# The modulation products of a two-stream trunk layer: VectorE multiply-adds behind the lead-in, column groups of TensorE in it

## The chip, the cores and the metric

One core of a Trainium2 chip. The metric is the time of one execution on the device in microseconds; the time before is the median of three runs.

## The reference, cut to what matters

One layer (D = 2048) runs over 128 context tokens and 256 sample tokens, T = 384 in all. Each stream has its own conditioning vector; both go through the same w_mod (2048 x 12288). The result is six rows of 2048 per stream: shift and scale for two norms, and two residual gates.

```python
m = silu(cvec) @ w_mod + b_mod                        # cvec: c_ctx for the context, c for the sample
hn = rmsnorm(x, g[0]) * (1.0 + mod[:, 1]) + mod[:, 0]
z = hn @ w_in                                         # 2048 x 5120
# x_lru, y_gate, b_g, c_g, v: convolution, gates, two scans, gated short convolution
x = x + mod[:, 2] * (concat(lru_out, sc_out) @ w_out) # 2048 x 2048
hn = rmsnorm(x, g[1]) * (1.0 + mod[:, 4]) + mod[:, 3]
f = (silu(hn @ w_gate) * (hn @ w_up)) @ w_down        # D_FF = 5632
x = x + mod[:, 5] * f
```

The outputs are both streams after a final rmsnorm and the last scan states of the context.

## The kernel before

**Products.** Activations lie transposed (features on partitions, 384 tokens in the free dimension). Every weight matrix is cut into blocks of 1024 elements a partition. A block arrives as fp32 in a `raw` slot; ScalarE rounds it to fp32r in `w_hi` (`round_blocks`, L427); VectorE subtracts, which gives the rest `w_lo` (`subtract_blocks`, L707); TensorE adds three products hi x hi, hi x lo, lo x hi (`product`, L1132 to L1134). A block of a large matrix is 24 matmuls of 384 columns (`gemm_block`). `w_hi` and `w_lo` have four slots, so block b can be rounded once TensorE is done with block b - 4. `raw` has four slots of 1 MB, two blocks each.

**Modulation.** w_mod is cut into 24 steps of 512 columns, each four quarters of 512 rows (1 MB). The two conditioning vectors are split into high and low parts, four stationary columns `cond_w`. A step is eight blocks; a block (`mod_block`, L1149) is four matmuls of 512 columns, so 32 a step, summed in rows 0 to 3 of `MOD_BANK`. VectorE copies the four rows to `mod_row` (`copy_row`, L713), TensorE turns them onto partitions and adds high and low with the matrix `select` (`turn_row`, L1166: four matmuls), and VectorE adds the bias into `modT` (`add_bias`, L719).

**Stages.** The lead-in holds product steps 0 to 7 (`mod_step`), which the first norm needs in full. In steps 1 to 4 x is transposed, the position embedding added (L821), and squares summed over features by matmuls against ones (L1221). Behind the root and its reciprocal (L734), POOL multiplies the eight pairs of tiles of x by it (L406). Then come 16 combined steps, GM 0 to 15 here (`gm_step`): ten over w_in (phases x, c, v, b, y, two steps each), four over w_out, one of w_gate and one of w_up. Each holds eight blocks of the large matrix, interleaved one to one with the eight blocks of one product step. In the w_in steps VectorE and ScalarE also do the convolutions (L849 to L858), gates and scans of one head a step (`powers`, `scans`); in the w_out steps the residual additions (L962) and sums of squares (L971). Steps 0 and 14 begin with a norm (`norm_tiles`, L762). Behind them the feed-forward runs in chunks without products.

**Order.** Every engine's order is written out by hand in one list per engine, with waits on counting semaphores: `lo_ready` (blocks subtracted), `block_done` (blocks used by TensorE), `landed` (per raw slot), `row_ready`, `row_turned`, `mod_ready`. SP issues all weight loads in order (L314). In a combined step even raw slots hold quarters of the large matrix and odd ones quarters of w_mod, and every load waits for `lo_ready`. In VectorE's list the row copy and the bias of step m stand in step m + 1.

Of the kernel before, what the change touches and what calls it, by code (L numbers as in the profile page):

```python
# [23 lines left out]
ALU = mybir.AluOpType  # L24
# [4 lines left out]
P = 128  # L29
# [34 lines left out]
def build(nc, x_prompt, x_sample, state_rglru, c, c_ctx, w_mod, b_mod, norm_g, w_in, lru_conv_w, lru_conv_b,  # L64
# [46 lines left out]
    N_IN = MOD_FIRST * 8  # L111
    N_OUT = N_IN + IN_STEPS * 16
    N_G0 = N_OUT + OUT_STEPS * 16
    N_U0 = N_G0 + 16
    N_G1 = N_U0 + 16
# [8 lines left out]
    with ExitStack() as ctx:  # L124
# [19 lines left out]
        mod_row = sb("mod_row", [4, BANK])  # L144
# [4 lines left out]
        cond_w = sb("cond_w", [P, KT, 4], F32R)  # L149
# [6 lines left out]
        state_rows = sb("state_rows", [2 * HEADS, P])  # L156
        select = sb("select", [4, 2])
# [54 lines left out]
        block_done = sem("block_done")  # L212
        zeroed = sem("zeroed")
# [5 lines left out]
        cond_hi_ready = sem("cond_hi_ready")  # L219
# [55 lines left out]
        def raw_of(kind, block):  # L275

            if kind == "GM":
                quad, at = divmod(block, 4)
                half, second = at % 2, at // 2
                wide = half == 1  # L280
            else:
                quad, at = divmod(block, 4)
                half, second = divmod(at, 2)
                wide = kind != "G"
            slot = 2 * (quad % 2) + half
            if not wide:
                return slot, raw[slot][:].rearrange("p (k n) -> p k n", n=256)[:, 4 * second:4 * second + 4, :]
            view = raw[slot][:].rearrange("p (k n) -> p k n", n=512)
            if kind == "D":
                return slot, view[:, :, 256 * second:256 * second + 256]  # L290
            return slot, view[:, 2 * second:2 * second + 2, :]

        def split_view(tile, kind, block):
            n = 512 if kind == "M" or (kind == "GM" and block % 2) else 256
            return tile[slot_of(block)][:].rearrange("p (k n) -> p k n", n=n)

        def landed_by(n, block):

            return (n - block) * 2 + 16 * (block // 8) + 16
# [5 lines left out]
        def _(sp):  # L305
            def quad(n, quad_at, halves, apart=False):


                first = 2 * (quad_at % 2)
                for half, source in enumerate(halves):  # L310
                    if not isinstance(n, int) or n >= 8:
                        sp.wait_ge(lo_ready, n - 6 + 2 * half if apart else n - 4)
                    width = source.shape[2]
                    sp.dma_start(raw[first + half][:].rearrange("p (k n) -> p k n", n=width), source)\  # L314
                        .then_inc(landed[first + half], 16)
# [5 lines left out]
            def mod_half(at, quarter):  # L321
                return w_mod_v[:, 4 * quarter:4 * quarter + 4, bass.ds(at, 512)]
# [5 lines left out]
            def gm_step(n, view, col, m, k_order=(0, 1)):  # L328
                at = held(m * 512)
                for q in range(4):  # L330
                    quad(n + 4 * q, q, [g_half(view, col, q, k_order), mod_half(at, q)])

            def g_step(n, view, col, apart=True):
                col = held(col)
                for q in range(2):
                    quad(n + 4 * q, q, [g_half(view, col, 2 * q), g_half(view, col, 2 * q + 1)], apart=apart)

            def d_step(n, chunk):
                first_k = held(chunk * CHUNK)
                for q in range(2):  # L340
                    quad(n + 4 * q, q, [w_down_v[:, bass.ds(first_k, CHUNK), 1024 * q + 512 * h:1024 * q + 512 * h + 512]
                                        for h in range(2)], apart=True)

            def m_step(n, m):
                at = held(m * 512)
                for q in range(2):
                    quad(n + 4 * q, q, [mod_half(at, 2 * q), mod_half(at, 2 * q + 1)], apart=True)

            m_step(0, 0)
# [3 lines left out]
            with sp.Fori(1, MOD_FIRST) as i:  # L353
                m_step(i * 8, i)
            for phase, (_, col) in enumerate(PHASES):
                with sp.Fori(0, 2) as i:
                    gm_step(i * 16 + N_IN + 32 * phase, w_in_v, i * 512 + col, i + (MOD_FIRST + 2 * phase))
            with sp.Fori(1, OUT_STEPS + 1) as i:
                gm_step(i * 16 + (N_OUT - 16), w_out_v, i * 512 - 512, i + (MOD_FIRST + IN_STEPS - 1), k_order=(1, 0))
            gm_step(N_G0, w_gate_v, 0, MOD_STEPS - 2)  # L360
            gm_step(N_U0, w_up_v, 0, MOD_STEPS - 1)
            g_step(N_G1, w_gate_v, 512, apart=False)
# [20 lines left out]
            sp.dma_start(new_state[0, 0].rearrange("a (h e) -> (a h) e", e=P), state_rows[:]).then_inc(stored, 16)  # L383
# [4 lines left out]
        def _(pool):  # L388
            for g, group in enumerate(groups[1:], 1):
# [6 lines left out]
            pool.dma_start(select[:], tables[0:4, POS + P:POS + P + 2]).then_inc(tables_landed, 16)  # L396
# [23 lines left out]
        def _(act):  # L420
            def round_blocks(kind, n, blocks):
                for b in blocks:
                    slot, source = raw_of(kind, b)
                    act.wait_ge(landed[slot], landed_by(n + b, b))
                    if not isinstance(n, int) or n + b >= SLOTS:
                        act.wait_ge(block_done, n + b - (SLOTS - 1))
                    act.activation(split_view(w_hi, kind, b), source, ACT.Copy).then_inc(hi_ready, 1)  # L427
# [27 lines left out]
            act.wait_ge(silu_ready, 1)  # L455
# [921 lines left out]
```

## Time and profile before

| | |
|---|---|
| median of three runs | 1910.89 us (1910.23 to 1910.91) |
| profiled execution, span of its core from first to last instruction | 1910.3 us |
| TensorE, VectorE, ScalarE, POOL busy | 1840.8, 1041.2, 794.7, 40.1 us |
| mean granted TensorE clock | 0.982 of full |
| DMA | 307.34 MB, mean 161 GB/s |
| lead-in | 0 to 131.9 us |
| combined steps GM 0 to 15 | 131.9 to 856.1 us |
| feed-forward and end | 856.1 to 1910.3 us |

The profiled execution's own time is given by its span; no separate time of it is listed beside the three runs. Step boundaries are read from the timeline: a step starts where VectorE's first subtraction of it has ended and TensorE takes up its first block. PE is TensorE's matmuls, PEld its weight loads; a matmul's duration overlaps the next one's, so starts are compared where a rate is meant. An fp32 matmul leaves two records, an fp32r matmul one.

### The profile page before, as it was taken

The page shows a single profiled execution, that of the slowest core. Times are in us where ns is not written, and L with a number is a line of the kernel's source. Part 1 is how long each engine was busy: PE and PEld are TensorE (multiplying, and loading weights), DVE is VectorE, ACT ScalarE, POOL GpSimd, SP SyncE. Part 2 cuts the span into 40 slices and gives each one's busy share as a digit, 9 for nine tenths or more (in the row PEclk, how much of TensorE's full clock was granted, in tenths as well). Part 3 has the DMA queues.
Part 4 walks back from the last instruction along what each step waited for, and adds up shares of the span by engine and source line. Part 5 has one row for each costly group of instructions (what it writes and reads, how often), then busy time and mean ns, then how long its engine had stood idle before and what let it go on. Part 6 is the DMA issues. An engine that isn't in the chain of part 4 may idle for free.

```text
span 1910.3 us, 25615 instructions
## 1 busy us (share of the span) xinstructions
PE 1840.8 (96%) x10189; PEld 1692.1 (89%) x10189; DVE 1041.2 (55%) x1380; ACT 794.7 (42%) x870; POOL 40.1 (2%) x43
## 2 busy tenths in 40 slices
PE   5979999999999998899999999999999999999997
PEld 2438888888888887789999999999999999999997
DVE  6887655775557556753434353535353534444445
ACT  5755455555676444642222222222222222222225
POOL 1040000000000000000000000000000000000000
PEclk9969999999999999999999999999999999999998
DMA  9956566556655565464333333433343334333321
GB/s 356 320 197 213 184 203 204 181 184 194 205 186 176 182 214 176 160 214 133 126 118 131 132 124 117 132 132 122 120 132 132 118 124 132 132 116 126 132 89 67
DMA packets 226464, 307.34 MB, mean 161 GB/s; under 512 B 5229, under 2 KB 152993, under 8 KB 226033
## 3 DMA queue, kind: packets, MB, share of 16 engines
q1 hardware_dynamic: 225008, 304.11, 46.8%
q0 software_dynamic: 1200, 2.52, 0.8%
q8 instruction: 29, 0.48, 0.1%
q14 instruction: 19, 0.15, 0.0%
q10 hardware_dynamic: 208, 0.08, 0.0%
HBM read 303.54 MB, written 3.15 MB: 161 GB/s over the span
## 4 chain that ended last, share of the span: by engine, by line
PE 89%; DVE 7%; ACT 2%; issue 1%; DMA 0%; ACTq 0%; DVEq 0%
PE psum L1132 26%; PE psum L1134 26%; PE psum L1133 26%; PE psum L1155 4%; PE psum L1156 4%; DVE w_lo L707 3%; PE psum L1166 1%; PE psum L1252 1%; ACT w_hi L427 1%; PE psum L1221 1%; DMA ident<-in_tables 0%; DVE act_lo L762 0%; DVE mod_row L713 0%; DVE scratch L747 0%; DVE scratch L918 0%
## 5 line engine op out<-in xcount | busy, mean ns | idle before, releaser
L707 DVE TENSOR_TENSOR w_lo<-raw,w_hi 128x1024 fp32r<-128x1024 f32 x568 | 695.7, 1243 | 820.7 <-ACT w_hi L427 819.8
L427 ACT ACTIVATE w_hi<-raw 128x1024 fp32r<-128x1024 f32 x568 | 587.5, 1056 | 1001.6 <-PE psum L1134 946.5
L1132 PE MATMUL psum<-act_hi,w_hi 128*128 128x384 f32 x2304 | 779.2, 338 | 20.2 <-DVE act_lo L762 15.2
L1134 PE MATMUL psum<-act_hi,w_lo 128*128 128x384 f32 x2304 | 773.6, 336 | 0.0
L1133 PE MATMUL psum<-act_lo,w_hi 128*128 128x384 f32 x2304 | 772.5, 335 | 0.0
L1132 PEld LDWEIGHTS psum<-act_hi,w_hi 128*128 128x128 f32 x2304 | 434.4, 189 | 42.7 <-issue 17.1
L1133 PEld LDWEIGHTS psum<-act_lo,w_hi 128*128 128x128 f32 x2304 | 434.5, 189 | 6.2
L1134 PEld LDWEIGHTS psum<-act_hi,w_lo 128*128 128x128 f32 x2304 | 434.0, 188 | 0.0
L1132 PE MATMUL psum<-h_hi,w_hi 128*128 128x384 f32 x704 | 235.7, 335 | 0.9 <-DVE h_lo L1025 0.9
L1134 PE MATMUL psum<-h_hi,w_lo 128*128 128x384 f32 x704 | 235.2, 334 | 0.0
L1133 PE MATMUL psum<-h_lo,w_hi 128*128 128x384 f32 x704 | 235.2, 334 | 0.0
L1155 PE MATMUL psum<-w_hi,cond_w 128*4 128x512 f32 x384 | 159.7, 416 | 24.4 <-DVE mod_row L713 17.0
L1156 PE MATMUL psum<-w_lo,cond_w 128*4 128x512 f32 x384 | 158.0, 411 | 0.0
L1132 PEld LDWEIGHTS psum<-h_hi,w_hi 128*128 128x128 f32 x704 | 132.1, 188 | 1.2 <-DVE h_lo L1025 1.2
L1133 PEld LDWEIGHTS psum<-h_lo,w_hi 128*128 128x128 f32 x704 | 132.2, 188 | 0.0
L1134 PEld LDWEIGHTS psum<-h_hi,w_lo 128*128 128x128 f32 x704 | 132.1, 188 | 0.0
L1034 DVE SCALAR_TENSOR_TENSOR xT<-psum,modT,xT 128x128 f32<-128x128 f32 x352 | 122.1, 409 | 7.0 <-PE psum L1134 6.9
L1155 PEld LDWEIGHTS psum<-w_hi,cond_w 128*4 128x4 f32 x384 | 33.2, 86 | 74.6 <-DVE w_lo L707 20.2
L1156 PEld LDWEIGHTS psum<-w_lo,cond_w 128*4 128x4 f32 x384 | 33.6, 87 | 47.5 <-issue 7.9
L613 ACT ACTIVATE h_hi<-stage 128x768 fp32r<-128x768 f32 x22 | 18.6, 846 | 48.1 <-DVE stage L1020 48.1
L1166 PEld LDWEIGHTS psum<-select,mod_row 4*128 4x128 f32 x192 | 23.9, 192 | 10.4 <-issue 8.7
L1166 PE MATMUL psum<-select,mod_row 4*128 4x2 f32 x192 | 25.9, 253 | 2.0 <-DVE mod_row L713 1.1
(129 smaller groups left out, 578.3 us busy)
## 6 DMA issues: line engine op xcount, KB each, us to landing
raw<-in_w_mod SPq DMA_DIRECT2D x96, 1024.0 KB, 7.3
raw<-in_w_gate SPq DMA_DIRECT2D x44, 1024.0 KB, 5.1
raw<-in_w_up SPq DMA_DIRECT2D x44, 1024.0 KB, 5.1
raw<-in_w_down SPq DMA_DIRECT2D x44, 1024.0 KB, 5.0
raw<-in_w_in SPq DMA_DIRECT2D x40, 1024.0 KB, 5.2
raw<-in_w_out SPq DMA_DIRECT2D x16, 1024.0 KB, 5.3
stage<-in_x_sample SPq DMA_DIRECT2D x2, 1024.0 KB, 15.9
y_sample<-stage SPq DMA_DIRECT2D x4, 512.0 KB, 4.7
```

What stands on the lines that cost most here:

```text
L427: act.activation(split_view(w_hi, kind, b), source, ACT.Copy).then_inc(hi_ready, 1)
L613: act.activation(h_hi[:, 2 * pair:2 * pair + 2, :], silu_g[:, 2 * pair:2 * pair + 2, :], ACT.Copy)\
L707: dve.tensor_tensor(split_view(w_lo, kind, b), source, split_view(w_hi, kind, b).bitcast(F32), ALU.subtract).then_inc(lo_ready, 1)
L1034: last = dve.scalar_tensor_tensor(xT[:, k, start:end], psum[:, down_banks[j] + a, start:end], modT[:, 5 * KT + k, seg:seg + 1], xT[:, k, s ...
L1132: pe.matmul(psum[:, bank, 0:T], hi, x_hi, start=first, stop=False)
L1133: pe.matmul(psum[:, bank, 0:T], hi, x_lo, start=False, stop=False)
L1134: return pe.matmul(psum[:, bank, 0:T], lo, x_hi, start=False, stop=last)
L1155: pe.matmul(psum[0:4, MOD_BANK, :], cond_w[:, k, :], hi[:, kk, :], start=k == 0, stop=False)
L1156: out = pe.matmul(psum[0:4, MOD_BANK, :], cond_w[:, k, :], lo[:, kk, :], start=False, stop=k == KT - 1)
L1166: out = pe.matmul(psum[:, SMALL_BANK, 2 * a:2 * a + 2], mod_row[:, a * P:(a + 1) * P], select[:], start=True, stop=True)
L1221: out = pe.matmul(psum[:, SUM_BANK, 0:T], ones[:], x_squares[:, a, :], start=four == 1 and a == 0, stop=four == 4 and a == 3)
L1252: out = pe.matmul(psum[:, bank, 0:T], gate_w[:, which, :], mix[:, bass.ds(head, 1), :].rearrange("p a t -> p (a t)"), start=True, stop=True)
```

## The change

- In the lead-in a product quarter is no longer rounded and split. TensorE reads the fp32 quarter from its raw slot with the unsplit fp32 `cond_w`, padded to 32 columns of which two are not zero. Its four 128-row pieces go to the four 32-column groups of the array and to four groups of 32 partitions of `MOD_BANK`: four fp32 matmuls of 512 columns a quarter, 16 a step. `copy_row` copies 128 partitions; `select` adds the groups.
- In the combined steps VectorE makes the products: `mod_quarter` multiplies and adds 4 x 2 times 512 elements a quarter into `mod_sum` (128 partitions, two streams), each waiting for the product before the last one. `turn_sum` sums over partitions with eight fp32 matmuls of one column against `ones`.
- A new semaphore `mod_used` counts used quarters. SP waits for it before it loads the next quarter into the slot.
- A combined step has 8 instead of 16 blocks to round and subtract, so the block counts and the places in all lists change. A memset of `cond_w` stands first in POOL's list.
- `state_rows` lies in `gate_w`, `mod_row` in `mod_sum`.

```diff
+            def load(slot, source):
+
+                width = source.shape[2]
+                sp.dma_start(raw[slot][:].rearrange("p (k n) -> p k n", n=width), source).then_inc(landed[slot], 16)
...
+                for q in range(4):
+                    slot = 2 * (q % 2)
+                    if first and q < 2:
+                        sp.wait_ge(mod_used, m * 4 - 4 + slot + 1)
+                    else:
+                        sp.wait_ge(lo_ready, n + (2 * q - 2))
+                    load(slot, g_half(view, col, q, k_order))
+                    if first and q < 2:
+                        sp.wait_ge(mod_used, m * 4 - 4 + slot + 2)
+                    else:
+                        sp.wait_ge(mod_used, m * 4 + (q - 1))
+                    load(slot + 1, mod_quarter(at, q))
...
+            def m_step(m):
                 at = held(m * 512)
+                for q in range(4):
+                    if not isinstance(m, int) or m:
+                        sp.wait_ge(mod_used, m * 4 + (q - 3))
+                    load(q, mod_quarter(at, q))
...
+            pool.memset(cond_w[:], 0.0).then_inc(cond_zeroed, 1)
...
+            def mod_quarter(m, q):
+
+                slot = 2 * (q % 2) + 1
+                dve.wait_ge(landed[slot], m * 32 + 16 * (q // 2 + 1 - MOD_FIRST))
+                rows = raw[slot][:].rearrange("p (k n) -> p k n", n=512)
+                if q:
+                    dve.wait_ge(mod_used, m * 4 + q)
+                for kk in range(4):
+                    k = 4 * q + kk
+                    for which in range(2):
+                        total, weight = mod_sum[:, which, :], cond[:, which, k:k + 1]
+                        if kk:
+                            dve.wait_ge(own.sem, own.value - 1)
+                        if k == 0:
+                            last = dve.tensor_scalar(total, rows[:, kk, :], weight, None, ALU.mult)
+                        else:
+                            last = dve.scalar_tensor_tensor(total, rows[:, kk, :], weight, total, ALU.mult, ALU.add)
+                        if kk < 3 or which == 0:
+                            own.add(last)
+                last.then_inc(mod_used, 1)
...
-                    subtract_blocks("GM", n, range(0, 2))
+                    subtract_blocks("GM", n, range(0, 1))
                     if head >= 1:
                         scans(head - 1)
...
+                    subtract_blocks("GM", n, range(1, 2))
+                    drain_pair(before, 2 * ((step - 1) % 2) + 1, 2, n)
+                    subtract_blocks("GM", n, range(2, 4))
+                    add_bias(m - 1)
+                mod_quarter(m, 0)
+                subtract_blocks("GM", n, range(4, 5))
+                mod_quarter(m, 1)
+                drain_pair(phase, 2 * turn, 0, n + 4)
+                subtract_blocks("GM", n, range(5, 7))
+                mod_quarter(m, 2)
                 if head >= 0:
                     powers(head)
-                subtract_blocks("GM", n, range(15, 16))
+                subtract_blocks("GM", n, range(7, 8))
+                mod_quarter(m, 3)
...
-            def mod_block(n, kind, b, k0):
...
+            def mod_quarter(q, slot, landing):
+
+                pe.wait_ge(landed[slot], landing)
+                rows = raw[slot][:].rearrange("p (k n) -> p k n", n=512)
+                for j in range(4):
+                    out = pe.matmul(psum[32 * j:32 * j + 32, MOD_BANK, :], cond_w[:, 4 * q + j, :], rows[:, j, :],
+                                    start=q == 0, stop=q == 3, tile_position=(0, 32 * j))
+                out.then_inc(mod_used, 1)
...
+            def turn_sum(m):
+
+                pe.wait_ge(mod_used, m * 4 + 4)
+                for a in range(4):
+                    for which in range(2):
+                        out = pe.matmul(psum[:, SMALL_BANK, 2 * a + which:2 * a + which + 1],
+                                        mod_sum[:, which, a * P:(a + 1) * P], ones[:, 0:1], start=True, stop=True)
+                out.then_inc(row_turned, 1)
```

The w_out, w_gate and w_up steps have the same pattern of quarters and blocks; step 0 and step 14 have their first quarter behind the norm tiles.

## Rows read from the trace of the kernel before

**Rows 1.** The page: busiest engine, and the chain that ended last.

```profile
PE 1840.8 (96%) x10189; PEld 1692.1 (89%) x10189; DVE 1041.2 (55%) x1380; ACT 794.7 (42%) x870; POOL 40.1 (2%) x43
...
PE 89%; DVE 7%; ACT 2%; issue 1%; DMA 0%; ACTq 0%; DVEq 0%
```

**Rows 2.** Windows of the lead-in: window, length, busy us per engine (x instructions), clock, DMA.

```profile
0.00:29.90 29.90, 10.14 (x36) 3.52 (x36) 14.46 (x33) 14.60 (x18) 6.66 (x18) 0.95 0.97 360
22.00:30.00 8.00, 0.79 (x5) 0.42 (x3) 4.84 (x23) 5.04 (x7) 0.00 (x0) 0.82 1.03 382
29.90:82.80 52.90, 49.50 (x232) 23.87 (x232) 45.30 (x57) 38.92 (x40) 0.75 (x1) 0.96 0.93 326
82.80:95.80 13.00, 11.38 (x48) 4.96 (x48) 11.27 (x10) 10.08 (x11) 0.00 (x0) 1.00 0.96 339
95.80:117.00 21.20, 14.57 (x36) 4.16 (x36) 21.01 (x9) 7.50 (x8) 21.16 (x9) 0.57 0.53 177
117.00:131.90 14.90, 13.14 (x45) 4.34 (x44) 11.16 (x12) 7.34 (x7) 1.46 (x2) 0.69 0.72 245
```

**Rows 3.** Windows behind it, columns as before: GM steps 0, 1, 2-3, 4-6, 7-8, 9-10, 11-13, 14, 15.

```profile
131.90:183.50 51.60, 46.53 (x245) 41.91 (x246) 40.40 (x58) 35.23 (x51) 0.00 (x0) 0.93 0.59 201
183.50:227.10 43.60, 43.60 (x240) 38.30 (x239) 30.62 (x41) 18.03 (x25) 0.00 (x0) 1.00 0.56 193
227.10:316.10 89.00, 89.00 (x482) 77.34 (x481) 55.37 (x68) 51.93 (x60) 2.88 (x4) 1.00 0.58 191
316.10:451.70 135.60, 133.99 (x722) 115.81 (x721) 96.39 (x138) 77.72 (x90) 4.31 (x6) 1.00 0.58 192
451.70:542.00 90.30, 90.11 (x486) 77.86 (x485) 54.28 (x63) 57.41 (x65) 2.88 (x4) 1.00 0.58 191
542.00:630.00 88.00, 84.17 (x450) 72.84 (x449) 57.04 (x65) 52.74 (x59) 0.00 (x0) 0.98 0.55 190
630.00:756.00 126.00, 126.00 (x698) 111.55 (x696) 73.76 (x92) 53.18 (x55) 0.00 (x0) 1.00 0.60 201
756.00:814.30 58.30, 45.69 (x237) 39.20 (x236) 43.43 (x58) 36.23 (x46) 0.00 (x0) 0.91 0.44 151
814.30:856.10 41.80, 41.80 (x233) 37.04 (x233) 21.46 (x20) 17.48 (x19) 0.00 (x0) 1.00 0.61 202
```

**Rows 4.** Timeline of TensorE, step 3: start us, length us; product matmuls.

```profile
273.26 0.40 PE L1155 MATMUL psum<-w_hi,cond_w 128*4 128x512 f32 x1
273.49 0.40 PE L1156 MATMUL psum<-w_lo,cond_w 128*4 128x512 f32 x1
```

**Rows 5.** Chain in order of time: row turning, and four fp32 matmuls (two records each).

```profile
46.48 2.58 PE psum L1221 x8
...
239.16 0.98 PE psum L1166 x8
```

**Rows 6.** Timeline near the end: three fp32 matmuls of one column.

```profile
1897.54 1.33 PE L1334 MATMUL psum<-ones,sumsq 128*128 128x1 f32 x6 [1.31 <-DVE sumsq L1105]
```

**Rows 7.** Groups by shape, VectorE: busy us, mean ns, idle before.

```profile
L707 DVE TENSOR_TENSOR w_lo<-raw,w_hi 128x1024 fp32r<-128x1024 f32 x568 | 695.7, 1243 | 820.7 <-ACT w_hi L427 819.8 <-DVE rstd L734 0.2
...
L713 DVE COPY mod_row<-psum 4x512 f32<-4x512 f32 x24 | 16.2, 674 | 3.1 <-PE psum L1156 3.0
...
L854 DVE SCALAR_TENSOR_TENSOR scratch<-scratch,prm 128x386 f32<-128x386 f32 x24 | 14.9, 621 | 0.8
...
L858 DVE SCALAR_TENSOR_TENSOR stage<-scratch,prm 128x256 f32<-128x256 f32 x16 | 7.7, 480 | 0.0
```

**Rows 8.** Timeline of VectorE, step 11: four multiply-adds of 128, 256, 128, 256 elements.

```profile
654.49 1.38 DVE L962 SCALAR_TENSOR_TENSOR xT<-psum,modT,xT 128x128 f32 x4
```

**Rows 9.** Timelines of POOL and of VectorE, end of the lead-in.

```profile
95.84 21.15 POOL L406 TENSOR_TENSOR stage<-xT,rstd 128x768 f32<-128x768 f32 x8 [18.14 <-DVE rstd L734]
...
99.25 18.82 DVE L707 TENSOR_TENSOR w_lo<-raw,w_hi 128x1024 fp32r<-128x1024 f32 x7
```

**Rows 10.** Timeline of VectorE, step 14: last norm tiles.

```profile
787.42 1.82 DVE L762 TENSOR_TENSOR act_lo<-scratch,act_hi 128x768 fp32r<-128x768 f32 x2
```

More of the change, by code:

```diff
@@ L305, in _, with mod_quarter @@
         def _(sp):
[L306 to L315, printed above, removed]
+            def load(slot, source):
+                width = source.shape[2]
+                sp.dma_start(raw[slot][:].rearrange("p (k n) -> p k n", n=width), source).then_inc(landed[slot], 16)
             def held(value):
                 return value if isinstance(value, int) else sp.snap(value)
-            def mod_half(at, quarter):
+            def mod_quarter(at, quarter):
                 return w_mod_v[:, 4 * quarter:4 * quarter + 4, bass.ds(at, 512)]
@@ L338, in d_step, with g_step @@
+            def g_step(n, view, col, first=False):
+                col = held(col)
+                for slot in range(SLOTS):
+                    if first and slot % 2:
+                        sp.wait_ge(mod_used, MOD_STEPS * 4 - 2 + slot // 2 + 1)
+                    elif first:
+                        sp.wait_ge(lo_ready, n - 2 + slot)
+                    else:
+                        sp.wait_ge(lo_ready, n + (2 * slot - 6))
+                    load(slot, g_half(view, col, slot))
             def d_step(n, chunk):
@@ L339, in d_step @@
                 first_k = held(chunk * CHUNK)
[L340 to L344, printed above, removed]
+                for slot in range(SLOTS):
+                    sp.wait_ge(lo_ready, n + (2 * slot - 6))
+                    load(slot, w_down_v[:, bass.ds(first_k, CHUNK), 512 * slot:512 * slot + 512])
@@ L504, in gelu @@
                     act.activation(gelu_y, banks(bank), ACT.Gelu_apprx_tanh).then_inc(gelu_ready, 1)
-                round_blocks("GM", n, range(0, 4 if step else 2))
+                round_blocks("GM", n, range(0, 2 if step else 1))
                 if step == 0:
@@ L975, in out_step @@
             def out_step(n, i, first):
-                subtract_blocks("GM", n, range(0, 3))
-                copy_row(None, n)
-                if not first:
-                    subtract_blocks("GM", n, range(3, 4))
+                subtract_blocks("GM", n, range(0, 2))
+                m = i + (MOD_FIRST + IN_STEPS)
                 if first:
@@ L1195, in turn_params, with mod_step @@
                                  ident[0:rows, 0:rows]).then_inc(turned, 1)
-            def mod_step(m, blocks=range(8)):
-                if blocks[0] == 0 and (not isinstance(m, int) or m):
+            def mod_step(m, quarters=range(4)):
+                if quarters[0] == 0 and (not isinstance(m, int) or m):
                     pe.wait_ge(row_ready, m)
-                for b in blocks:
-                    mod_block(m * 8 + b, "M", b, 2 * b)
-                    if b == 4 and (not isinstance(m, int) or m):
+                for q in quarters:
+                    mod_quarter(q, q, m * 16 + 16)
+                    if q == 2 and (not isinstance(m, int) or m):
                         turn_row(m - 1)
```

322 lines of the change are left out of this document (144 added, 178 removed).

## The prediction

> **What bounds the kernel now.** I read the page first, then the chain of waits, then windows cut at the steps, then shapes and single timelines. On the page TensorE is busy 96% of the span and the chain that ended last lies on it for 89% [rows 1]. That average hides two regimes, and the windows separate them. In the lead-in (0 to 131.9 us, product steps 0 to 7) DMA is busy over 90% until 95.8, so the loads almost set the pace; then comes a stretch at 53% with a granted clock of 0.57 [rows 2]. There POOL's eight multiplications take 21.15 us and VectorE needs 18.82 us for seven subtractions, 2.7 us each instead of 1.24: the two slow each other, TensorE waits, and DMA waits with it [rows 7, 9]. Behind the lead-in the 16 combined steps (GM 0 to 15) run from 131.9 to 856.1 with TensorE busy nearly throughout, VectorE between 51% and 78% [rows 3]. From 856.1 to the end nothing changes except one row turning.
>
> The sum is made against the profiled execution, span 1910.3 us; the median of the three runs is 1910.89, 0.6 above, which I add at the end.
>
> **TensorE behind the lead-in.** A step loses 32 product matmuls. They start 0.23 us apart [rows 4], so 7.4 us. Its row turning (four matmuls, 0.98 us [rows 5], 0.245 each) becomes eight one-column matmuls against ones. No row shows eight in a stream. Below, the price of the four turning matmuls gives 8 x 0.245 = 1.96; above, three such matmuls took 1.33 us [rows 6], so 3.5. The turning is nearest in being pipelined, so 1.96. TensorE needs 6.4 us less a step.
>
> **VectorE behind the lead-in.** A step loses eight subtractions and one row copy and gains 32 products of 128x512, 30 of them multiply-adds. No row has that width. Multiply-adds of 386 and 256 elements last 0.621 and 0.480 us [rows 7], 1.085 ns an element, so 512 elements last 0.758. What counts in a queue is start to start. Four multiply-adds took 1.38 us, the last a 256-element one of 0.48: three starts in 0.90 for 512 elements, or 0.556 for elements and 0.115 fixed for each [rows 8, 7]. So 0.556 + 0.115 = 0.67 us a product. Each waits only for the product before the last (two accumulators alternate), which ended before it could start. Bounds: 0.60 (nearly no fixed part) and 0.79 (0.758 and a semaphore's turn). 32 x 0.67 = 21.4 us; off go 8 x 1.15 (1.243 less the same overlap of 0.09) and 0.6 for the copy: VectorE needs 11.6 us more a step. The two products of a step that are plain multiplications may save 0.5; I leave that for lost handovers.
>
> The Trainium skill's page "VectorE: DVE Perf Modes", section "The DRAIN you can't avoid", says that the next operation does not start until the pipe is empty. Here the four in rows 8 are shorter together than their durations, so the trace speaks against a full drain; by the rule a product costs 0.758, and that is the second rival below.
>
> **Step by step**, the larger of VectorE (busy + 11.6 a step) and TensorE (busy - 6.4 a step) [rows 3]:
> - step 1: 30.6 + 11.6 = 42.2, before 43.6;
> - steps 2-3: 55.4 + 23.2 = 78.6 (TensorE 76.2), before 89.0;
> - steps 4-6: 96.4 + 34.8 = 131.2, before 135.6. Two convolution drains a step make VectorE the bound; TensorE idles in lumps of some 6 us;
> - steps 7-8: 77.5 (TensorE 77.3), before 90.3;
> - steps 9-10: 80.2, before 88.0;
> - steps 11-13: 108.6 (TensorE 106.8), before 126.0.
>
> That is 518.3 against 572.5: 54 us off. Half of what TensorE gets back is lost again, because VectorE arrives at the same moment.
>
> Step 0 gets longer. VectorE's 40.4 + 11.6 = 52.0, and about 3.5 at its start when it waits for the row to be turned and for ScalarE's first scaled tile: 55.5 against 51.6, +4. There the products queue behind the norm tiles and ahead of blocks 4, 5 and 7 of the weights.
>
> Step 14 has a serial head (sum of squares, root, norm tiles) that stays. Its last norm tile ends at 789.2 [rows 10]; three subtractions and the row copy fewer ahead of it make that 785.2. Then 21.4 of products, four subtractions (4.6) and step 15's first (1.15) give 812.4 against 814.3: 2 off. Step 15 has VectorE 33.1, TensorE 35.4 against 41.8: 6 off. The next turning costs 1 more.
>
> **Queues.** SP's loads of product quarters now wait for VectorE's products and stand in front of weight loads. Walked through: blocks 6 and 7 of a step are issued once its first quarter is used, some 8 us before their rounding; 1.05 MB takes 2.7 us at full rate [rows 2], two of them 5.5. It fits, with 1 to 2 us to spare. ScalarE loses eight roundings a step and was no bound (35.2 of 51.6 at most [rows 3]); it hides at nothing behind TensorE. POOL gets a memset ahead of its parameter loads; I take up to 1 us at the first row, covered by the loads under way.
>
> **The lead-in.** It must load eight product steps and x: 8 x 4.19 + 3.15 = 36.7 MB. By 29.9 us 10.8 MB are in [rows 2]. The full rate is 382 GB/s (window 22 to 30, share 1.03). The other 25.9 MB take 67.8 us: 97.7. A quarter frees its slot as soon as TensorE has used it, no rounding or subtraction between, so I let the rate hold, with 1.5 for a gap where step 1 starts, 0.9 for the last quarter and 2 for stretches at the lower clock: the last row is complete at 102 instead of 131.9, 30 off. A quarter is four fp32 matmuls of 512 columns; four of 384 take 2.58 us in all [rows 5], 0.645 each, so 0.86. If the four column groups run together a quarter takes 0.86, otherwise 3.44. The loads bring a quarter each 2.7. No row shows column groups. The same skill's page "TensorE: Matmul & The Clock Gate", Part 3, gives a measured 2.38x for three column tiles; by that a quarter would take about 1.5, an estimate, and the sum stays. POOL is ready: step 5 starts near 66 instead of 82.8, POOL began 13.0 behind that start [rows 2, 9], and its 21.15 (less, uncontended) end by 100.
>
> **Sum:** 30 - 4 + 54 + 2 + 6 - 1 = 87 off 1910.3 is 1823.3; with 0.6, 1824.
>
> **Rivals.**
> 1. The column groups do not run together: the change doesn't do what it says there. A quarter is 3.44, a step 13.8. Steps 1 to 4 add the x work, (49.5 - 4 x 7.4) / 4 = 5.0 each [rows 2], 18.8; steps 5 to 7 add 1 of turning and once 2.6 of squares, 47.0. From 29.6 the row is complete at 151.8, 50 later than forecast: 1874. For it: no fp32 matmul in column groups in the trace. 14%.
> 2. A product costs its full 0.758: 0.088 x 32 = 2.8 us a step; in step 15 TensorE hides it, so 15 x 2.8 = 42 more, 1866; at 0.79 it would be 58, 1882. Against: rows 8. 16%.
> 3. Slower than before. In the lead-in the groups run one after the other and the clock stays at its lower level, as it fell to 0.57 and 0.69 where TensorE waited on others [rows 2]. A quarter is then T = 6.9, and the other work of rival 1 doubles: the row is complete at 29.6 + 28 T + 40 + 11 = 274, 172 later than forecast, and the kernel takes 1996. All that is won elsewhere is 57, so this decides from a last row at 189, T = 3.9 us, on. Against it: an engine that computes all the time had a clock of 1.00 [rows 3]. 4%.
> 4. Better: a product at 0.60 takes 2.2 off each step that VectorE bounds and leaves TensorE the bound in steps 2, 3, 7, 8 and 11 to 13 (22 in all), and the lead-in runs without its 3.5 of allowance: 1798.
>
> **Numbers.** Forecast (1798 to 1850, the products between 0.60 and 0.72, rival 4 at its end) 64%, rival 1 14%, rival 2 16%, rival 3 4%, anything else that leaves no gain 2%. The range 1800 to 1878 takes in the forecast and rivals 1 and 2 in most of their width. The measurement tells about 0.2% (4 us) from no change. Faster 0.95, same 0.01, slower 0.04.
>
> **What would show it.** Lead-in windows at 370 GB/s or more and first norm near 102; fp32 product matmuls of a quarter starting together and ending within 0.9 us (else rival 1); products 0.67 apart, 32 a step, VectorE over 90% in steps 1 to 13; steps of about 39 in 2, 3, 7, 8, of 46 to 47 in step 5; TensorE idle before blocks 5 and 7 in steps 4 to 6, released by subtractions; the part behind 856.1 unchanged in length. Wrong would be: TensorE's clock low for long after those idle lumps, or SP's loads late so that ScalarE's rounding waits on DMA.

## The result and the profile after

The changed kernel takes 1934.8 us (median of four runs, 1933.7 to 1935.7) against 1910.6 for the one before in the same runs: a ratio of 1.0124, interval 1.011 to 1.0138. It is slower by 24 us where 87 less was forecast. The two profiled executions, spans 1934.0 and 1910.3, are compared below.

The page of the changed kernel: busy time and chain, to be read beside [rows 1].

```profile
PE 1750.1 (90%) x9805; PEld 1676.3 (87%) x9805; DVE 1125.9 (58%) x1683; ACT 602.9 (31%) x678; POOL 33.7 (2%) x44
...
PE 68%; DVE 17%; DMA 7%; issue 5%; ACT 3%; SPq 0%; DVEq 0%; ACTq 0%
```

TensorE has 91 us less to do, VectorE 85 us more, and neither is full: the chain goes back and forth between them. The windows say where (columns as in [rows 2, 3]): two of the lead-in, then GM steps 0, 1, 2-3, 4-6, 7-8, 9-10, 11-13, 14, 15. Here each is cut where TensorE starts a step's first block; step 13 so includes the head of the second norm.

```profile
22.00:95.00 73.00, 57.11 (x328) 24.50 (x328) 15.07 (x38) 10.18 (x10) 14.86 (x9) 0.80 1.04 382
95.00:111.40 16.40, 7.94 (x45) 3.43 (x41) 4.64 (x12) 4.14 (x7) 1.52 (x3) 0.60 1.07 366
111.40:159.10 47.70, 40.13 (x192) 39.49 (x193) 45.38 (x70) 21.55 (x32) 0.00 (x0) 0.82 0.49 159
159.10:207.20 48.10, 40.80 (x213) 39.81 (x212) 40.10 (x63) 10.89 (x20) 0.00 (x0) 0.89 0.56 184
207.20:301.10 93.90, 81.71 (x435) 77.55 (x433) 75.15 (x109) 37.05 (x46) 2.88 (x4) 0.95 0.54 180
301.10:449.70 148.60, 122.17 (x651) 113.80 (x649) 128.08 (x207) 53.61 (x66) 4.31 (x6) 0.94 0.53 174
449.70:544.00 94.30, 81.96 (x433) 77.15 (x433) 75.66 (x109) 41.23 (x49) 2.88 (x4) 0.95 0.56 184
544.00:638.40 94.40, 78.23 (x420) 75.16 (x420) 82.13 (x120) 37.20 (x43) 0.00 (x0) 0.95 0.55 178
638.40:787.50 149.10, 116.79 (x643) 112.07 (x643) 115.43 (x178) 34.63 (x39) 0.00 (x0) 0.93 0.56 183
787.50:834.70 47.20, 37.97 (x193) 35.82 (x193) 44.15 (x65) 22.92 (x30) 0.00 (x0) 0.93 0.41 133
834.70:879.10 44.40, 37.65 (x209) 36.49 (x209) 31.81 (x44) 9.94 (x10) 0.00 (x0) 0.96 0.58 191
```

Cut in the same way, the kernel before begins step 0 at 138.0 and leaves step 15 at 856.1; the changed one does so at 111.4 and 879.1. So the lead-in gave 26.6 us, the sixteen steps took 49.6 more (767.7 instead of 718.1), and the rest is as long as it was (1054.9 and 1054.2). All of the loss lies in the combined steps, where 58 less was forecast. In steps 1 to 13 and 15 neither TensorE (78 to 87% busy) nor VectorE (72 to 87%) has a busy time near the window's length: that points to a handover, not a volume. Steps 0 and 14 are different: there VectorE is busy 45.4 of 47.7 and 44.2 of 47.2 us.

The waits of the changed kernel in the combined steps 1 to 13, 159 to 780 us (who waited for whom: us in total, times, longest):

```profile
PE psum L1160 <- DVE w_lo L718: 91.3, 47, 7.0
DVE modT L751 <- PE psum L1201: 83.1, 13, 8.4
```

VectorE waits once a step at the bias (L751) for the row to be turned (L1201), 6.4 us each time in the mean, and TensorE then waits for subtractions. One round of it, from step 3 of the changed kernel: the timeline of VectorE, that of SP, and of TensorE the first large matmul of the next step (timeline) and the next turning (chain in order of time):

```profile
268.85 0.17 DVE L751 TENSOR_TENSOR modT<-psum,prm 128x8 f32<-128x8 f32 x1 [6.88 <-PE psum L1201]
268.93 0.87 DVE L740 TENSOR_SCALAR mod_sum<-raw,cond 128x512 f32<-128x512 f32 x2
269.72 4.06 DVE L742 SCALAR_TENSOR_TENSOR mod_sum<-raw,cond,mod_sum 128x512 f32<-128x512 f32 x6
273.70 1.22 DVE L718 TENSOR_TENSOR w_lo<-raw,w_hi 128x1024 fp32r<-128x1024 f32 x1
...
284.07 1.22 DVE L718 TENSOR_TENSOR w_lo<-raw,w_hi 128x1024 fp32r<-128x1024 f32 x1 [1.85 <-ACT w_hi L443]
...
294.10 5.39 DVE L742 SCALAR_TENSOR_TENSOR mod_sum<-raw,cond,mod_sum 128x512 f32<-128x512 f32 x8
299.40 1.22 DVE L718 TENSOR_TENSOR w_lo<-raw,w_hi 128x1024 fp32r<-128x1024 f32 x1
...
307.67 1.23 DVE L718 TENSOR_TENSOR w_lo<-raw,w_hi 128x1024 fp32r<-128x1024 f32 x1 [0.27 <-ACT w_hi L443]
315.77 0.17 DVE L751 TENSOR_TENSOR modT<-psum,prm 128x8 f32<-128x8 f32 x1 [6.87 <-PE psum L1201]
```

```profile
273.94 0.37 SPq L306 DMA_DIRECT2D raw<-in_w_mod  x1
274.56 0.37 SPq L306 DMA_DIRECT2D raw<-in_w_in  x1
```

```profile
301.10 0.63 PE L1160 MATMUL psum<-act_hi,w_hi 128*128 128x384 f32 x1
...
314.05 1.69 PE psum L1201 x16
```

Read it as a loop. `mod_quarter(m, 0)` overwrites `mod_sum`, which `turn_sum(m - 1)` reads; so the bias and the first product stand behind the turning. From the bias at 268.85 VectorE works through four quarters of products and four subtractions to the next step's first subtraction, done at 300.6: 31.8 us. TensorE is through with the old step and with the gate matmuls at about the same time, starts block 0 at 301.1, is done with blocks 0, 1 and 2 at 314.05 (13.4 us after VectorE's subtraction) and turns the row until 315.74, 1.7 us. Only then does VectorE go on: 31.8 + 13.4 + 1.7 = 46.9, the length of the step (from bias to bias, 268.85 to 315.77). VectorE's subtractions and scans beside TensorE's three blocks fill only part of the 13.4, and TensorE's blocks 3 to 7 are fed one by one behind products. Both engines are on the path, one after the other.

### The profile page after: what moved, and what is told of

The parts are those of the page before. It is cut to its first block, busy times and chain, and to the rows that moved or that the text cites. A ratio compares the mean times of both kernels' runs of the same rounds, so it can differ in the third digit from the quotient of the medians.

```text
span 1934.0 us, 24719 instructions
## 1 busy us (share of the span) xinstructions
PE 1750.1 (90%) x9805; PEld 1676.3 (87%) x9805; DVE 1125.9 (58%) x1683; ACT 602.9 (31%) x678; POOL 33.7 (2%) x44
## 4 chain that ended last, share of the span: by engine, by line
PE 68%; DVE 17%; DMA 7%; issue 5%; ACT 3%; SPq 0%; DVEq 0%; ACTq 0%
PE psum L1160 22%; PE psum L1161 21%; PE psum L1162 21%; DVE mod_sum L742 9%; DMA raw<-in_w_in 3%; DMA raw<-in_w_mod 3%; DVE w_lo L718 2%; PE psum L1201 1%; PE psum L1182 1%; ACT w_hi L443 1%; DVE mod_sum L740 1%; ACT scratch L457 1%; DVE scratch L872 1%; DMA raw<-in_w_gate 0%; ACT act_hi L461 0%
## 5 line engine op out<-in xcount | busy, mean ns | idle before, releaser
L1160 PE MATMUL psum<-act_hi,w_hi 128*128 128x384 f32 x2304 | 797.8, 346 | 132.0 <-DVE w_lo L718 112.3
L718 DVE TENSOR_TENSOR w_lo<-raw,w_hi 128x1024 fp32r<-128x1024 f32 x376 | 458.3, 1224 | 596.1 <-ACT w_hi L443 595.4
L1161 PE MATMUL psum<-act_lo,w_hi 128*128 128x384 f32 x2304 | 787.0, 342 | 0.0
L1162 PE MATMUL psum<-act_hi,w_lo 128*128 128x384 f32 x2304 | 786.4, 341 | 0.0
L443 ACT ACTIVATE w_hi<-raw 128x1024 fp32r<-128x1024 f32 x376 | 394.6, 1058 | 998.8 <-PE psum L1162 687.1
L1160 PEld LDWEIGHTS psum<-act_hi,w_hi 128*128 128x128 f32 x2304 | 445.5, 193 | 156.9 <-DVE w_lo L718 126.0
L1161 PEld LDWEIGHTS psum<-act_lo,w_hi 128*128 128x128 f32 x2304 | 446.0, 194 | 0.5
L742 DVE SCALAR_TENSOR_TENSOR mod_sum<-raw,cond,mod_sum 128x512 f32<-128x512 f32 x480 | 323.3, 745 | 0.0
L751 DVE TENSOR_TENSOR modT<-psum,prm 128x8 f32<-128x8 f32 (+1 forms) x24 | 4.0, 166 | 128.2 <-PE psum L1201 94.2
L1182 PE MATMUL psum<-raw,cond_w 128*32 128x512 f32 x256 | 43.5, 783 | 23.8 <-DMA raw<-in_w_mod 19.0
L1182 PEld LDWEIGHTS psum<-raw,cond_w 128*32 128x32 f32 x256 | 6.5, 124 | 47.4 <-DMA raw<-in_w_mod 19.7
L624 ACT ACTIVATE h_hi<-stage 128x768 fp32r<-128x768 f32 x22 | 18.6, 846 | 48.1 <-DVE stage L1041 48.1
L1201 PEld LDWEIGHTS psum<-ones,mod_sum 128*128 128x128 f32 x256 | 30.8, 192 | 1.2 <-DVE mod_sum L742 1.2
```

Of the source, the lines that this page charges most:

```text
L443: act.activation(split_view(w_hi, b), source, ACT.Copy).then_inc(hi_ready, 1)
L718: dve.tensor_tensor(split_view(w_lo, b), source, split_view(w_hi, b).bitcast(F32), ALU.subtract).then_inc(lo_ready, 1)
L742: last = dve.scalar_tensor_tensor(total, rows[:, kk, :], weight, total, ALU.mult, ALU.add)
L1160: pe.matmul(psum[:, bank, 0:T], hi, x_hi, start=first, stop=False)
L1161: pe.matmul(psum[:, bank, 0:T], hi, x_lo, start=False, stop=False)
L1162: return pe.matmul(psum[:, bank, 0:T], lo, x_hi, start=False, stop=last)
```

## The experiments

Each is one edit of the changed kernel unless it says otherwise; before was measured beside each at 1910.7 to 1911.6.

**1. Where the row is turned.** The turning moves from ahead of the 4th block to ahead of the 1st, 2nd or 3rd.

```diff
-            def gm_step(n, m, bank_free, acts=None, k_order=(0, 1), turn_at=3, gates=None, pair_banks=(0, 2)):
+            def gm_step(n, m, bank_free, acts=None, k_order=(0, 1), turn_at=0, gates=None, pair_banks=(0, 2)):
```

> The changed kernel with one edit: TensorE turns the previous step's row ahead of a combined step's first block instead of ahead of its fourth. Theory A (VectorE's bias waits for that turning, 6.9 us in each step, and the first product quarter and all behind it are late by as much): steps 2 and 3 fall from 46.9 to about 40, the wait before the bias (94 us in all) falls below 20, and the kernel takes about 1855 (1840 to 1875). Theory B (loads of blocks 6 and 7 stand in SP's queue behind the wait for the first product quarter): the stall moves to the rounding, gain under 20, above 1915. Theory C (VectorE has more work in a step than TensorE, throughput): the wait before the bias was slack that VectorE would need anyway, gain under 20.

> The changed kernel with the turning ahead of a step's third block instead of its fourth: half of the dose of the run that turns first. Theory A (each block ahead of the turning is 4.2 us that VectorE waits in each of 13 steps): 13 x 4.2 = 54 less than the changed kernel, about 1880 (1870 to 1890), between it and the 1840 of turning first. Theory B (loads) or a threshold in the queue: no change by itself, or all of the gain at once.

> One edit against the changed kernel: the row of the step before is turned ahead of the 2nd block (the change has it ahead of the 4th; the 3rd gave 1876.6 us, the 1st 1840.5). Theory (VectorE stands still at the bias until the row is turned, and TensorE's block is 4.2 us, so each block the turning moves forward takes 4.2 us off a wait of 6.9 us): 2.7 us of wait were left ahead of the 3rd block and none is left ahead of the 2nd; and ahead of the 1st block TensorE waits for VectorE's last product (7.7 us in 159 to 780), which the block now ahead of the turning covers. So 1835 us (1828 to 1842). Rival (what counts is that the row is handed over as early as can be, since VectorE needs all the lead that it can get): between the two neighbours, about 1856 (1848 to 1866).

| turned ahead of block | median us | ratio, interval | bias waits | TensorE waits for w_lo |
|---|---|---|---|---|
| 4th (the change) | 1934.8 | 1.0124, 1.011 to 1.0138 | 83.1 | 91.3 |
| 3rd | 1876.6 | 0.9816, 0.980 to 0.9833 | 29.7 | 55.7 |
| 2nd | 1840.6 | 0.9636, 0.962 to 0.9653 | 1.6 | 36.3 |
| 1st | 1840.5 | 0.9627, 0.9611 to 0.9643 | none | 23.7 |

The waits are those of 159 to 780 us, row for row. For the 3rd and the 2nd block:

```profile
PE psum L1160 <- DVE w_lo L718: 55.7, 30, 5.0
DVE modT L751 <- PE psum L1201: 29.7, 10, 4.2
```

```profile
PE psum L1160 <- DVE w_lo L718: 36.3, 28, 4.5
DVE modT L751 <- PE psum L1201: 1.6, 1, 1.6
```

Each block of some 4.2 us that the turning moves forward comes off the bias's wait until that is gone, and the kernel gets 58, 36 and 0 us faster. A handover moved by one argument is worth 94 us. The 1st place came out 15 us better than the theory's 1855, at the edge of its range; the 3rd fell near its 1880. The 2nd place fell where the theory put it (1828 to 1842), not at the rival's 1856.

**2. The load order.** SP issues the last weight load of a step (blocks 6, 7) ahead of the load of the third product quarter, which waits for VectorE to use the first one.

```diff
+                weights(2)
+                weights(3)
+                products(2)
+                products(3)
```

(in place of weights and products in turn; the first two pairs stay as they are)

> The changed kernel with one edit: SP issues the load of blocks 6 and 7 ahead of the load of the third product quarter, so it no longer waits until VectorE has used the first quarter. Theory A: only the 1.9 us that the subtraction of block 6 waited go away, 1915 to 1930. Theory B: the steps lose the 8.4 us load from their chain, below 1890. Theory C: no change, 1930 to 1937.

> Both edits of the two runs before. Theory A: as with the turning alone or up to 10 us better, 1840 to 1865, VectorE busy over 90% in steps 1 to 9. Theory B: most of the gain of this run was there with the load order alone. Theory C: still above 1915.

> The same place for the turning (ahead of the 2nd block), and with it the load order of the second experiment (the last weight load of a step ahead of the load of the third product quarter). With the turning ahead of the 1st block the load order took another 10.3 us off. Theory as for the run beside it: 10 less than that one, 1825 us (1818 to 1832), so 5 below the version with both edits. Rival: 1846 (1838 to 1856).

(SP then issues the loads in the order W0 P0 W1 P1 W2 W3 P2 P3, W for weights, P for products.) Alone it gives 1920.4 us (ratio 1.0044, 1.0027 to 1.0061), 14 less than the change; with the turning ahead of the 1st block 1830.2 (0.9575, 0.9559 to 0.9591), 10 less than that alone; ahead of the 2nd 1831.9 (0.9587, 0.9571 to 0.9603), 9 less. Of the forecasts, that for the load order alone held (1915 to 1930); with the turning ahead of the 1st block the "up to 10 us" held, but the 1830.2 lies below the range of 1840 to 1865, because the turning alone had already come out at its lower end. The load is the one issued at 274.56 above, once VectorE had used up the first quarter at 273.7; the chain in order of time of the changed kernel gives its length, and ScalarE's waits for such loads (159 to 780 us) are of the changed kernel first and of the load order alone second:

```profile
274.56 8.39 DMA raw<-in_w_in
282.98 1.06 ACT w_hi L443
```

```profile
ACT w_hi L443 <- DMA raw<-in_w_in: 197.1, 25, 19.9
```

```profile
ACT w_hi L455 <- DMA raw<-in_w_in: 83.6, 21, 15.6
```

It takes 8.4 us, and VectorE's next subtraction waits 1.85 for it. In the changed kernel a load of 1 MB that has the DMA engines to itself takes 4.9 to 5.3 us from issue to landing (the one issued at 258.64 landed at 263.73). Issued 0.6 to 0.8 us behind a product quarter, as in steps 9 and 11 to 13, a weight load takes 7.2 to 7.3. In steps 2 to 8 two loads of 128 KB of gate weights, issued by POOL (here at 274.68 and 275.40), are under way as well, and it takes 8.3 to 9.0. The bias's wait hardly changes with the load order alone (82.2 against 83.1), so this is a second, smaller loss beside the first. The turning ahead of the 2nd block is no better than ahead of the 1st once the loads are in order: the theory had 1825 (1818 to 1832), 5 below the version with both edits; measured it is 2 above, at the end of the range.

**3. Volume against place.** 448 of the 512 columns of each product behind the lead-in are left out (not added up); the products keep their number, waits and loads (`rows` is cut to the same 64 columns, and the second half of `mod_sum` is set to zero once at the start). Once with the turning ahead of the 1st block, once ahead of the 4th.

```diff
-                        total, weight = mod_sum[:, which, :], cond[:, which, k:k + 1]
+                        total, weight = mod_sum[:, which, 0:64], cond[:, which, k:k + 1]
```

> Leaves out 448 of the 512 columns of each product behind the lead-in (they are not added up). Row turned ahead of the first block as in the first experiment (1840.5 us); the products' volume on VectorE then almost goes (a product of 64 columns about 0.07 + 0.115 = 0.19 us start to start instead of 0.67, so 15 us less a step), while waits, turning, bias and loads stay. Theory (with the turning ahead of the first block what is left over is VectorE's volume and not a handover): the steps fall to what TensorE needs, 36 to 38 each, and the kernel to 1790 us (1775 to 1805). Rival (the steps are held by handovers or by loads that arrive late, not by volume): above 1820.

> The changed kernel with the row turned where it has it (ahead of the 4th block), and 448 of the 512 columns of each product behind the lead-in left out (they are not added up). It completes a square of place and volume: 1934.8 (4th, full), 1840.5 (1st, full), 1782.6 (1st, short). Theory (the late turning costs time only because what VectorE has behind the bias, some 31 us, is as long as the rest of the step; with 22 us of it gone TensorE's own blocks cover the wait): the place costs nothing any more, 1784 us (1776 to 1795), so of the 94 us between the places all hang on the volume. Rival (the wait for the turned row costs by itself, whatever VectorE has to do): 5 to 7 us a step remain, 1850 us or more.

Ahead of the 1st block it takes 1782.6 us (1778.0 to 1784.8), ahead of the 4th 1818.4 (1814.6 to 1820.9). With the turning first, 58 us of the kernel's time hang on VectorE's volume, as the theory had it: steps 2 and 3 last 37.7, TensorE's own pace (192 large matmuls 0.173 apart, 1.7 of turning, 2.6 of gates). Ahead of the 4th, neither theory holds. The late place still costs 36 us with most of the volume gone (1784 was expected), though far less than 94. What is left is in the waits and the chain of that kernel:

```profile
DVE modT L751 <- PE psum L1202: 104.3, 14, 10.3
```

```profile
251.81 0.37 SPq L306
252.43 8.36 DMA raw<-in_w_in
260.81 1.06 ACT w_hi L443
```

The bias waits longer than ever (159 to 780 us), and TensorE covers most of that (it waits 27.5 us for w_lo); but the first product quarter is used late too, its slot is freed late, and the weight load queued behind that slot's reload on SP is issued late and lands 8.4 us after its issue. So the late turning acts in two ways: VectorE stands still, and a transfer behind it starts late. The square shows 36 us for what does not need the volume and 58 for what does. How the 36 divide between the load and TensorE's own waits was not tried (it would need the short products with experiment 2's order).

**4. Where the products are made.** The same quarters in the combined steps on TensorE's column groups, as in the lead-in: first in all sixteen steps, then, on top of experiments 1 and 2, in steps 0, 5, 10 and 14 alone, where VectorE is the bound: in the version with both edits it is busy there 46.6 of 49.9, 46.3 of 46.9, 42.8 of 43.7 and 44.8 of 45.2 us.

```diff
+                    if b % 2:
+                        if b == 1:
+                            pe.wait_ge(row_ready, m)
+                        q = b // 2
+                        mod_quarter(q, 2 * (q % 2) + 1, m * 32 + 16 * (q // 2 + 1 - MOD_FIRST))
```

(behind each `gemm_block`; `turn_row` instead of `turn_sum`, `copy_row` one step later, and VectorE's `mod_quarter` away; the mixed version makes this hang on the step, and turns the row after such a step ahead of the 3rd block)

> The changed kernel, with the products of the combined steps too as unsplit fp32 in four column groups of TensorE (a quarter behind every second block; rows copied and turned as in the lead-in), nothing of them on VectorE. A quarter took 1.06 us in the lead-in at the full clock, so a step holds 33.3 of blocks, 4.2 of products, 1.0 of turning and in nine of them 2.6 of gates: 38.5 to 41.1 against 42.0 and 44.5 in the kernel before, with no idle TensorE. With the 26 us of the lead-in that gives 1830 to 1840. If the array has to empty when it changes between groups and full width, each quarter costs up to 0.5 more at each side: 64 x 1.0, about 1895.

> Both edits (turning first, weights' load first), and in the four combined steps where VectorE is the bound (0, 5, 10 and 14) the products on TensorE in column groups. By the steps' lengths in the two runs, 41.3 for 49.9, 41.6 for 46.9, 39.5 for 43.7 and 41.7 for 45.2: 22 us less than with both edits alone, about 1808 (1800 to 1820). If a step's length hangs on its neighbours, so that VectorE's work is only shifted: 1820 to 1830.

> Against the mixed version (1824.2 us): the step that follows each of the four group steps copies the row right behind its first subtraction and turns it ahead of the second block instead of the third. In the mixed version those steps (1, 6, 11, 15) lasted 44.1, 41.3, 40.2 and 37.8 us against 39.7, 40.7, 38.3 and 33.4 with sums throughout, 11.4 more in all. Theory (VectorE's list stands still at the bias until the row is turned, so the earlier the turning the shorter the wait): these 11 go almost all, 1813 us (1810 to 1819). Rival (those steps are longer because the group step hands over no finished blocks ahead, wherever the row is turned): no change, 1821 to 1827. Rival 2 (the row copy ahead of the second subtraction holds up TensorE's second block as much as it gains): 1820 to 1828.

Groups in every step: 1836.2 us (0.9608, 0.9592 to 0.9624), as forecast; the 1895 of an array that has to empty at each change fell. A stretch of two such steps, window 197 to 280:

```profile
197.00:280.00 83.00, 83.00 (x481) 72.17 (x480) 39.76 (x55) 36.80 (x45) 2.88 (x4) 1.00 0.64 209
```

TensorE is full at a clock of 1.00, a step is 41.6, and VectorE has room: the bias waits (63.7 us in 159 to 780) and costs nothing in this stretch. One quarter is 1.06 us (eight records); the same work costs VectorE 5.4. This version without a product on VectorE lies within 5 us of the best place for the turning in the change.

The mixed version takes 1824.2 (0.9548, 0.9532 to 0.9564), the fastest but for the one below. The theory had 1808 (1800 to 1820) and fell; its rival, that VectorE's work is only shifted to the neighbours (1820 to 1830), held. Steps 0, 5, 10 and 14 fall from 49.9, 46.9, 43.7 and 45.2 to 42.1, 41.2, 39.5 and 41.7, 21 us in all where 22 were reckoned, but the steps behind them grow by 4.4, 0.6, 1.9 and 4.4. The last experiment copied and turned the row earlier in those: 1820.9 (0.9532, 0.9515 to 0.9549), where the theory had 1813 (1810 to 1819) and the rival that the place of the turning does not matter 1821 to 1827: the theory fell, and the two rivals of the expectation lie too close together to be told apart. Its VectorE in step 1:

```profile
154.44 0.69 DVE L742 COPY mod_sum<-psum 128x512 f32<-128x512 f32 x1 [7.37 <-PE psum L1210]
155.05 1.22 DVE L736 TENSOR_TENSOR w_lo<-raw,w_hi 128x1024 fp32r<-128x1024 f32 x1
```

The wait had moved from the bias to the copy: the group step's last quarter stands at the end of TensorE's list for that step, and VectorE, which would run ahead into the next step, now cannot. Intervals overlap, so that this version is faster than the mixed one is not shown; both beat before and the change.

**5. Do the groups run together?** All pieces of a lead-in quarter in one column group, one after the other (copying and turning the row then take 32 partitions).

```diff
-                    out = pe.matmul(psum[32 * j:32 * j + 32, MOD_BANK, :], cond_w[:, 4 * q + j, :], rows[:, j, :],
-                                    start=q == 0, stop=q == 3, tile_position=(0, 32 * j))
+                    out = pe.matmul(psum[0:32, MOD_BANK, :], cond_w[:, 4 * q + j, :], rows[:, j, :],
+                                    start=q == 0 and j == 0, stop=q == 3 and j == 3, tile_position=(0, 0))
```

> The changed kernel, but all four product matmuls of a quarter in the lead-in go to one column group, one after the other. If the four groups ran together in the changed kernel, a quarter goes from 1.06 to 3.4 us or more, above the 2.7 us in which its load arrives, and the last row is complete near 150 instead of 104: about 1980. If the groups bring nothing, no change: 1934.

1990.8 us (one run), 56 more than the change; step 0 starts at 167.2 instead of 111.4, and behind it the steps are as long as in the change (767.1 us for the sixteen). One quarter in four groups (changed kernel, timeline of TensorE at clock 1.00), then in one:

```profile
78.80 1.07 PE L1182 MATMUL psum<-raw,cond_w 128*32 128x512 f32 x8 [0.66 <-DMA raw<-in_w_mod]
```

```profile
87.00 3.62 PE L1182 MATMUL psum<-raw,cond_w 128*32 128x512 f32 x8
```

3.6 us against 1.07: four groups run 3.4 times as fast as one. The forecast had 3.44 and 0.86.

## Why the prediction was wrong, point by point

**The step that failed** is "Step by step, the larger of VectorE and TensorE". It takes the two engines as running beside each other, each with its volume. The description of the kernel before named the ordering ("the row copy and the bias of step m stand in step m + 1") and never priced the turning's place in the new loop: a product that overwrites what the turning reads makes VectorE wait for TensorE's third block, while TensorE waits for VectorE's first subtraction. In step 3 this path is 46.9 us long, where the sum had 39.3. The sum's volumes were near. TensorE needs 38.5 us a step where it is not held up (steps 2 and 3 with both edits, 77.1 us of the window's 77.1), and 38.1 was reckoned. VectorE's busy time in steps 1 to 13 grew by 136.7 us (379.8 before, 516.6 in the change), 10.5 a step where 11.6 was reckoned. With the turning moved (experiment 1, first place) and cut as above, the steps came out like this; the last column adds the load order:

| GM steps | before | forecast | the change | turned first | and loads in order |
|---|---|---|---|---|---|
| 0 | 43.4 | 47.4 | 47.7 | 50.0 | 49.9 |
| 1 | 42.9 | 41.5 | 48.1 | 39.7 | 39.7 |
| 2, 3 | 89.0 | 78.6 | 93.9 | 78.3 | 77.2 |
| 4 to 6 | 135.6 | 131.2 | 148.6 | 131.2 | 129.7 |
| 7, 8 | 89.6 | 76.8 | 94.3 | 78.6 | 76.4 |
| 9, 10 | 91.8 | 84.0 | 94.4 | 83.5 | 84.0 |
| 11 to 13 | 137.5 | 120.1 | 149.1 | 127.2 | 127.2 |
| 14 | 46.3 | 44.3 | 47.2 | 48.5 | 45.2 |
| 15 | 41.9 | 35.9 | 44.4 | 36.1 | 33.4 |
| all | 718.1 | 660 | 767.7 | 673.1 | 662.8 |

(The forecast column is before less the forecast's gain for those steps.) Steps 11 to 13 alone stay 7 us above their forecast. The other rows miss by up to 2.5 us to either side, so part of the total's closeness (3 us) is that they cancel.

**Queues: "it fits, with 1 to 2 us to spare".** Wrong: 5.5 us were reckoned for two loads, both at full rate. One load alone lands 5.1 us after its issue, although 1 MB takes 2.7 at full rate, so 2.4 were left out; two in a row land 7.9 us after the first issue (564.18 to 572.12), and in steps with gate weights 9.0 (273.94 to 282.96). Worth 14 us in the change, 9 to 10 with the turning moved.

**A product at 0.67 us.** Right. In the timeline of step 3 six products take 3.98 us to the next operation's start (269.72 to 273.70), 0.66 each, where each lasts 0.745:

```profile
L742 DVE SCALAR_TENSOR_TENSOR mod_sum<-raw,cond,mod_sum 128x512 f32<-128x512 f32 x480 | 323.3, 745 | 0.0
L740 DVE TENSOR_SCALAR mod_sum<-raw,cond 128x512 f32<-128x512 f32 x32 | 14.0, 480 | 0.0
```

Rival 2 falls with it. The Trainium skill's page "VectorE: DVE Perf Modes", section "The DRAIN you can't avoid", says that the next operation starts only when the pipe is empty, and then that one that is not held starts earlier. The prediction took up only the first of these; this stream, where each starts 0.08 ahead of the recorded end of the one before, agrees with the second.

**The turning at 1.96 us.** 1.69 measured (eight matmuls, sixteen records); 0.27 too high.

**The lead-in, 30 off.** Nearly right: rate 382 GB/s held for 73 us (window above), the last row was copied at 103.6 instead of 102, and TensorE's first block came at 111.4 instead of 138.0: 26.6. The copy is 28 earlier than it was; the remaining two went into the wait for the first weight load, issued at 95.4, landed at 104.9 as the chain has it:

```profile
93.43 1.97 PE psum L1182 x8
95.42 9.45 DMA raw<-in_w_in
104.90 1.06 ACT w_hi L443
```

A quarter took 1.04 to 1.08 us where 0.86 was forecast (1.92 for two in a row), and 1.9 at the lower clock, both less than the 2.7 us in which the loads bring one. Rival 1 falls by experiment 5. The Trainium skill's page "TensorE: Matmul & The Clock Gate", Part 3, has 2.38x for three column tiles; here four give 3.4x for one quarter and, for two in a row, 7.05 us (98.99 to 106.04 in experiment 5) against 1.92 (66.52 to 68.44 in the change), 3.7x. Rival 3, the slower one, came out with the right sign and the wrong place: it lay in the lead-in, which was a gain.

**POOL.** 14.2 us for its eight multiplications instead of 21.15 [rows 9], 1.8 us each, in a stretch where VectorE is busy 15 of 73 us. As forecast, no longer in the way.

**The range and the chances.** Slower had 4%, all of it on a mechanism in the lead-in. A wait for another engine in the middle of a step was in none of the cases. The prediction did name two signs that it would be wrong, and both came: TensorE's clock low behind idle lumps (in short stretches, the last section has one), and ScalarE's rounding waiting on DMA (197.1 us above; the combined steps of the kernel before have no such wait). The sign for the handover itself (the bias waiting on the turning) it did not name.

## What to carry to other kernels

A step is as long as its engines' volumes only if no engine waits in its middle for something that another does after waiting for it. When work moves to another engine, follow each buffer that it overwrites to its reader, see where that reader stands in its own engine's list, and add up the path once around the loop; if that is longer than the larger volume, move the reader before anything else. Then ask which load is queued behind the slot that the moved work now frees late.

## What the runs showed of the hardware that was not expected

Behind short waits of TensorE stand slow matmuls, so that a wait can cost more than its length. In step 3 of the changed kernel it waited 1.90 us for a subtraction (to 294.24), and within the block that followed its matmuls start 0.32 us apart instead of 0.17. Timeline of TensorE, then the window of that stretch, whose clock column says 0.50, the lower of the two levels (here 1.2 GHz):

```profile
294.24 0.44 PE L1160 MATMUL psum<-act_hi,w_hi 128*128 128x384 f32 x1 [1.90 <-DVE w_lo L718]
...
296.04 0.52 PE L1160 MATMUL psum<-act_hi,w_hi 128*128 128x384 f32 x1
296.37 0.52 PE L1161 MATMUL psum<-act_lo,w_hi 128*128 128x384 f32 x1
...
299.39 0.34 PE L1162 MATMUL psum<-act_hi,w_lo 128*128 128x384 f32 x1
```

```profile
295.90:299.20 3.30, 3.30 (x12) 3.30 (x11) 3.30 (x6) 0.00 (x0) 0.00 (x0) 0.50 0.87 299
```

From the 3071 distances between the starts of the 3072 large matmuls of the sixteen steps: in the changed kernel 302 follow their forerunner by 0.25 to 0.36 us instead of 0.173, 41 us more in all; in the kernel before 43 do, 6 us; with the turning ahead of the 1st block 178, 25 us. That gives an account of the 50 us in these steps (windows 138.0 to 856.1 before and 111.4 to 879.1 in the change). TensorE is busy 62 us less (637.4 for 699.8), which is 97 us of work taken away and 35 us added by slower matmuls; and it idles 112 us more (130.3 for 18.3). So the 49.6 us are 112 + 35 - 97. Not all of that comes on top of the waits: the block around 296 lost 1.6 us in this way, but the next step's first block could not start before VectorE's subtraction at 300.6 anyway, and started at 301.1. How much would remain at full clock was not tried.
